# Router on unnormalised rows, modulation folded into its weights, reordered start, RWKV products and end

## The reference, cut to what matters

```python
mod = silu(c) @ w_ada + b_ada
sh1, sc1, gt1, sh2, sc2, gt2 = split(mod, 6)
h = rms_norm(x, norm1_g) * (1 + sc1) + sh1
y = hybrid_mixer(h, ...)          # RWKV-7 | mLSTM | window attention, gated, @ w_out
x = x + gt1 * y                   # x1 below
h = rms_norm(x, norm2_g) * (1 + sc2) + sh2
x = x + gt2 * hier_moe(h, ...)    # 32 experts, 4 groups, top 2 in the best group
# in hier_moe
g_prob   = softmax(h @ w_rg + b_rg);  g_top, g_idx = top_k(g_prob, 1)
e_logits = (h @ w_re + b_re).reshape(NT, 4, 8)   # those of group g_idx are used
```

## Time and profile before

| | before |
|---|---|
| median of 3 runs | 1950.85 us (1950.84 to 1951.01) |
| the profiled execution | 1950.37 us, its span 1948.6 us |
| PE busy | 1815.5 us, 93% of the span |
| DVE, ACT, POOL busy | 664.9, 438.4, 233.9 us |
| moved by DMA | 334.18 MB, mean 171 GB/s |
| the chain that ended last | PE 88%, DMA 4%, DVE 3%, ACT 2% |

### The profile page before, as it was taken

The page is one execution under the profiler, slowest core; times in us unless marked ns, Lnnn a source line. Parts: engine busy times, 40 slices in busy tenths (PEclk is TensorE's granted clock), DMA queues, the critical chain, the costliest instruction groups (busy, mean ns, idle before and its releaser), DMA issues.

```text
span 1948.6 us, 37426 instructions
## 1 busy us (share of the span) xinstructions
PE 1815.5 (93%) x16145; PEld 1014.4 (52%) x16145; DVE 664.9 (34%) x1569; ACT 438.4 (23%) x999; POOL 233.9 (12%) x352
## 2 busy tenths in 40 slices
PE   6999999999994999999999999996999999999990
PEld 3455445555442555555555554554566656655550
DVE  4385425554445233323332334553111001110014
ACT  4220412222334122211222131112222212222110
POOL 3030001000100122022201231001000000000003
PEclk9999999999997999999999999997999999999995
DMA  9386001001211001011010156224999999999988
GB/s 315 115 279 235 22 22 33 22 22 33 65 54 41 17 15 31 17 31 26 19 31 17 57 189 238 97 113 149 389 393 401 395 391 389 384 395 387 386 318 327
DMA packets 146930, 334.18 MB, mean 171 GB/s; under 512 B 19275, under 2 KB 63225, under 8 KB 146845
## 3 DMA queue, kind: packets, MB, share of 16 engines
q1 hardware_dynamic: 127776, 282.68, 40.0%
q0 software_dynamic: 8240, 25.04, 3.9%
q10 hardware_dynamic: 10828, 25.24, 3.3%
HBM read 299.50 MB, written 37.63 MB: 173 GB/s over the span
## 4 chain that ended last, share of the span: by engine, by line
PE 88%; DMA 4%; DVE 3%; ACT 2%; issue 1%; POOL 1%; SPq 1%; ACTq 0%; POOLq 0%; DVEq 0%
PE bank L285 83%; DMA arena<-in_w_e_in 3%; PE bank L1214 1%; POOL arena L718 1%; PE bank L885 1%; DMA arena<-y_slots,ints 1%; PE bank L1231 1%; SPq L457 0%; PE bank L1233 0%; PE bank L1153 0%; DMA y_slots<-arena 0%; DVE arena L1788 0%; DVE arena L1877 0%; PE bank L761 0%; ACT arena L1345 0%
## 5 line engine op out<-in xcount | busy, mean ns | idle before, releaser
L285 PE MATMUL bank<-arena 128*32 128x256 f32 (+8 forms) x15294 | 1726.3, 378 | 37.4 <-DVE arena L1877 6.3
L285 PEld LDWEIGHTS bank<-arena 128*32 128x32 f32 (+4 forms) x15294 | 924.8, 133 | 779.2 <-issue 522.5
L2232 DVE TENSOR_TENSOR arena<-arena,bank 128x128 f32<-128x128 f32 x96 | 21.9, 283 | 369.8 <-ACT arena L1631 369.8
L1618 ACT ACTIVATE arena<-bank,arena 128x96 f32<-128x96 f32 x256 | 85.9, 441 | 12.0 <-PE bank L1214 12.0
L682 POOL DMA_INDIRECT arena<-xnorm,ints x32 | 31.6, 986 | 471.1 <-PE bank L1214 466.7
L2241 DVE TENSOR_TENSOR arena<-bank,arena 128x512 f32<-128x512 f32 x64 | 35.7, 558 | 132.9 <-PE bank L285 132.9
L1624 ACT ACTIVATE arena<-bank 128x384 f32<-128x384 f32 x32 | 15.7, 490 | 267.7 <-PE bank L1233 267.7
L2025 DVE TENSOR_TENSOR arena<-arena,bank 128x256 f32<-128x256 f32 x40 | 16.8, 421 | 172.8 <-PE bank L285 172.8
L633 POOL TENSOR_TENSOR arena<-arena 64x256 f32<-64x256 f32 x96 | 71.2, 741 | 28.3 <-DVE arena L2011 21.7
L1569 ACT ACTIVATE arena<-bank 128x256 f32<-128x256 f32 (+1 forms) x48 | 18.3, 382 | 208.7 <-PE bank L285 208.7
L1631 ACT ACTIVATE arena<-bank 128x128 f32<-128x128 f32 x96 | 19.7, 278 | 164.6 <-PE bank L285 164.6
(11 more groups left out here) (330 smaller groups left out, 1013.2 us busy)
## 6 DMA issues: line engine op xcount, KB each, us to landing
arena<-in_w_e_in SPq DMA_DIRECT2D x64, 2048.0 KB, 22.1
arena<-in_w_e_out SPq DMA_DIRECT2D x32, 2048.0 KB, 22.1
arena<-in_w_ada SPq DMA_DIRECT2D x12, 2048.0 KB, 12.7
arena<-in_w_in SPq DMA_DIRECT2D x32, 512.0 KB, 3.9
y_slots<-arena ACTq DMA_DIRECT2D x32, 288.0 KB, 6.3
y_slots<-arena POOLq DMA_DIRECT2D x21, 384.0 KB, 17.5
arena<-in_x SPq DMA_DIRECT2D x4, 1024.0 KB, 8.3
arena<-in_w_in SPq DMA_DIRECT2D x2, 2048.0 KB, 25.0
```

The lines of the kernel that those rows point to most:

```text
L285: return nc.tensor.matmul(o, l, r, start=start, stop=stop)
L1618: ins = A.activation(e_xT[s][:, k, :], PS[k // 4][:, ts(k % 4, CAP)], ACT.Identity, scale=sc2[:, k:k + 1], bias=sh2[:, k:k + 1])
L2232: ins = TT(e_h[:, r, :], e_g[:, r, :], E_GU[r][:, P:2 * P], ALU.mult)
```

## The change

- Start: the copies of the transposed tiles 0 to 3 stand between ACT's squares; gate row 2 directly behind row 0; the copies of tiles 4 to 7 are all ACT's; DVE makes the products of slice 1 ahead of `norms(1)`.
- RWKV: the four products with `a_wr` together, then the four with `a_qs`.
- Router: transposes read `o_x` itself and wait for `o_x1`. `wr` is multiplied by `sc2` once; `ones` times (`wr` x `sh2`), eight matmuls in bank 2, is added to `br`; the norm factor `rstd` multiplies the logits. The copies to `o_hT` are plain. The update is added in two halves. SP's load into `o_x` also waits for the transposes.
- Tail: `place` and `table` of tile 6 before the last route; ranks of tile 6 in bank 0; the first two gathers read the table without a copy; DVE makes half of expert 0's `e_xT`.
- End: the x1 loads wait for `win_used` instead of `y`; POOL itself waits for the stores of y; ACT reads the number of extra blocks ahead of its last store.

```diff
@@ names
-        VECS, MOD1 = range(1, 3)
+        VECS, MOD1, WR_SHIFT, WR_SCALE, WR_BIAS = range(1, 6)
@@ rank_bank
-            return PS[6][:, 64:64 + NE] if t < NT - 1 else PS[4][:, 0:NE]
+            return PS[6][:, 64:64 + NE] if t < NT - 2 else PS[4 * (t - NT + 2)][:, 0:NE]
@@ sync
                     sp.wait_ge(sem("x_norm"), NT + t - 1)
+                    sp.wait_ge(sem("x_used"), NT + t - 1)
...
-            sp.wait_ge(sem("y"), 2 * (NE - 1))
+            sp.wait_ge(sem("win_used"), NE - 1)
             for t in range(NT):
                 sp.dma_start(f_x[t], x1_t[t]).then_inc(sem("gate_in"), 16)
@@ gpsimd, gather(e, s, wait)
-                G.tensor_copy(i_ix[s], i_tab[:, ds(e, 1)]).then_inc(sem("ix_set"), 1)
-                pool.wait_ge(sem("ix_set"), e + 1)
                 if wait:
+                    G.tensor_copy(i_ix[s], i_tab[:, ds(e, 1)]).then_inc(sem("ix_set"), 1)
+                    pool.wait_ge(sem("ix_set"), e - 1)
                     pool.wait_ge(sem("xs_used"), e - 1)
...
             pool.wait_ge(sem("extra_end"), 1)
+            for s in range(2):
+                pool.wait_ge(sem(f"y_st{s}"), 32 * NE // 2)
@@ tensor
             ada_row(0)
+            ada_row(2)
             for t in range(4, NT):
                 x_transposes(t)
-            ada_row(2)
...
-                for h in range(H):
-                    a, p = h % 2, h // 2
-                    rows = slice(64 * a, 64 * a + 64)
-                    mm(PS[3 + a][:, ts(p, N)], a_wr[rows, p, :], a_st[rows, p, :])
-                    ins = mm(PS[3 + a][rows, ts(2 + p, N)], a_qs[rows, p, :], a_st[rows, p, :])
+                for p in range(2):
+                    for a, rows in enumerate(halves):
+                        mm(PS[3 + a][:, ts(p, N)], a_wr[rows, p, :], a_st[rows, p, :])
+                for p in range(2):
+                    for a, rows in enumerate(halves):
+                        ins = mm(PS[3 + a][rows, ts(2 + p, N)], a_qs[rows, p, :], a_st[rows, p, :])
                 ins.then_inc(sem("a_Y"), 1)
...
             pe.wait_ge(sem("mix_done"), 2 * NT + NT)
+            pe.wait_ge(sem("setup_dve"), WR_SHIFT)
+            for k in range(KT):
+                ins = mm(PS[2][:, 0:36], ones, r_lg[:, k, :], k == 0, k == KT - 1)
+            ins.then_inc(sem("gates_pe"), 1)
...
             def transposes(t):
-                pe.wait_ge(sem("x_norm"), NT + t + 1)
+                pe.wait_ge(sem("o_x1"), t + 1)
...
             for t in range(NT):
+                if t == 0:
+                    pe.wait_ge(sem("setup_dve"), WR_BIAS)
...
             logits(NT - 1)
+            table(NT - 2)
             ranks(NT - 1)
...
-            table(NT - 2)
             table(NT - 1)
@@ scalar
             for t in range(4):
                 squares(t + 4)
+                x_out(t)
             A.activation(ss[:, 4:8], ss[:, 4:8], ACT.Sqrt, scale=1.0 / D, bias=EPS).then_inc(sem("x_ss"), 1)
-            for t in range(4):
-                x_out(t)
...
+                A.activation(o_hT[:, 0:4, :], PS[4].rearrange("p (k n) -> p k n", k=4), ACT.Copy).then_inc(sem("xT_a"), 1)
...
-            xT_out(0, 0)
+            xT_out(0, 0, 4)
...
-            store(NE - 1, 1)
-            for s in range(2):
-                act.wait_ge(sem(f"y_st{s}"), 32 * NE // 2)
             act.wait_ge(sem("router_dve"), EXTRAS)
             n_extra = act.value_load(i_ex[0:1, NX:NX + 1], min_val=0, max_val=NX)
             act.wait_ge(sem("slots_zero"), 16 * NX)
-            act.sem_inc(sem("extra_go"), 1)
+            store(NE - 1, 1)
@@ vector
-            norms(1)
             dve.wait_ge(sem("setup_act"), COND)
             ada(1)
-            for t in range(4, NT):
-                x_out(t)
+            norms(1)
             ada(3)
...
+            TT(r_lg, wr, bc(sh2, 36), ALU.mult).then_inc(sem("setup_dve"), 1)
+            dve.wait_ge(sem("setup_dve"), WR_SHIFT)
+            TT(wr, wr, bc(sc2, 36), ALU.mult).then_inc(sem("setup_dve"), 1)
...
+            dve.wait_ge(sem("gates_pe"), 5)
+            TT(br, br, PS[2][:, 0:36], ALU.add).then_inc(sem("setup_dve"), 1)
...
+                V.tensor_copy(o_hT[:, 4:8, :], PS[5].rearrange("p (k n) -> p k n", k=4)).then_inc(sem("xT_v"), 1)
+                if t == NT - 1:
+                    place(NT - 2)
                 dve.wait_ge(sem("r_mm"), t + 1)
-                TT(r_lg[:, t, :], PS[6][:, 0:36], br, ALU.add).then_inc(sem("r_lg"), 1)
+                STT(r_lg[:, t, :], PS[6][:, 0:36], rstd[:, t:t + 1], br, ALU.mult, ALU.add).then_inc(sem("r_lg"), 1)
```

More of the change, by code:

```diff
@@ L1266, in _ @@
             pe.wait_ge(sem("xs1_in"), 16)
-            pe.wait_ge(sem("e_xT"), 1)
             xT(1, 1)
@@ L1348, in x_out @@
                 act.wait_ge(sem("x_used"), t + 1)
-                A.activation(HT[:, 0:4, ts(t, P)], PS[2 * (t % 2)].rearrange("p (k n) -> p k n", k=4), ACT.Copy)\
-                    .then_inc(sem("xT_a"), 1)
+                for j in range(1 if t < 4 else 2):
+                    ins = A.activation(HT[:, 4 * j:4 * j + 4, ts(t, P)], PS[2 * (t % 2) + j].rearrange("p (k n) -> p k n", k=4), ACT.Copy)
+                ins.then_inc(sem("xT_a"), 1)
             for t in range(4):
@@ L2163, in _ @@
             route(NT - 1)
-            place(NT - 2)
             place(NT - 1)
@@ L2241, in y_out @@
                     TT(e_y[s][:, cols], PS[5 + u][:, 0:(512, 256)[u]], gt2[:, cols], ALU.mult).then_inc(sem("y_out"), 1)
+            dve.wait_ge(sem("xs_used"), 1)
+            for k in range(4, KT):
+                ins = TS(e_xT[0][:, k, :], PS[1][:, ts(k - 4, CAP)], sc2[:, k:k + 1], sh2[:, k:k + 1], ALU.mult, ALU.add)
+            ins.then_inc(sem("xT_v"), 1)
             activate(0)
```

57 lines of the change are left out of this document (32 added, 25 removed).

## The result

The changed kernel takes 1920.2 us (median of 6 runs, 1918.35 to 1921.95), the kernel before 1950.8 (median of 6, 1948.54 to 1951.01): ratio 0.9848, 95% interval 0.9839 to 0.9858. Forecast were 1927.9 and a range of 1924 to 1936. The profiled execution took 1921.71 us, its span 1919.8; that of before 1950.37 and 1948.6. The table cuts both spans at the same seven events, so a stretch is the time from one event to the next. Its times are starts of rows of PE's, SP's and POOL's timelines and of the chain of waits, before and after.

A forecast was written before the change was run, and what follows sets the result against it. PE was taken to bound the chunks, w_out loop and experts, a chain over several engines the router tail and end. -3.4 - 12.0 + 3.55 - 0.8 - 4.7 - 5.6 = -22.95 gave 1927.9 us as median, range 1924 to 1936.

The forecast's parts named there:

- What bounds the kernel: PE is busy nearly throughout RWKV chunks, w_out loop and experts, so its savings there move the end one for one.
- Part 2: RWKV chunks: grouped state products take 0.96 us instead of 2.47 per chunk, 1.5 x 8 chunks, -12.0 us.
- rival A: RWKV chunks: `a_wr` products do not overlap, or only form changes are saved; -4.9 to -8, 1932 to 1935; chance 0.12.
- all terms at their better ends: Whole kernel: every term comes out at its favourable bound, giving 1924 us; chance 0.04.
- Rival C: Merges and on: narrow matmuls and short stalls leave PE's clock at 1.2 GHz; slower, 1976 us; chance 0.03.
- A clock of 0.5 in the merges: Merges after the RWKV chunks: PE showing this granted clock would mean the forecast is wrong.
- Part 1: Start, up to the first projection: gate row 0 starts at 22.4 us instead of 25.87, -3.4 us.
- Part 3: Router weights, merges to w_out: eight added matmuls +2.0, waits +0.35 and +1.2, sum +3.55 us; separately -0.8 in the loop.
- The shorter copies were covered too: w_out loop: plain copies to `o_hT` save nothing, because w_out matmuls already hide them.
- Part 4: Router tail, last w_out matmul to first expert matmul: -2.5, -0.7, -0.3 and -1.2, sum -4.7 us.
- Part 5: End: last store of y lands sooner without x1 loads beside it, -4.5, ACT's part -1.1; sum -5.6 us.
- Loads of the experts: Experts: DMA share is 1.03, but PE's progress releases the loads, so they move with PE's start.

The follow-up runs named there:

- state_undone: The changed kernel with the old order of the state products (`a_wr` and `a_qs` alternating) in the RWKV chunks: 1938.19 us, ratio 0.9941 to the kernel before.
- state_alone: The kernel before with only the new order of the state products (four `a_wr`, then four `a_qs` per RWKV chunk): 1929.13 us, ratio 0.9890.
- narrow_split: The kernel before, old order kept, with two of eight 512-column matmuls moved from behind the state products to ahead of them: 1949.10 us, ratio 0.9998.

## Why the prediction was wrong

**What bounds the kernel.** Right that the chunks move the end one for one. The failing step stands here: the row 638 to 1146 us has a clock of 0.98, and I read only its busy column. A mean of 0.98 over 508 us is 0.02 x 508 = 10 us of full-speed work lost. The five falls are 17 us at 1.2 GHz, which is 8.5 us of it; the rest is the end of the slow stretch ahead of chunk 1, and rounding.

**Part 2.** The term "-12.0" was right for what it priced, 8 x 1.50, and rival A is out: the products with `a_wr` do run in pairs. The term was mis-sized, because it left out that the removed stretch also cost the clock behind it, which the sum put at nothing. The chunks gave 19.5 us in this trace, 7.5 more than the term; by the totals it is 6.0 (state_undone, 18.0 - 12.0) to 9.2 (state_alone, 21.2 - 12.0). That is why the time lies below the range. The range was also cut short by its own terms: -14 for `a_wr` at 0.045 comes to 13.2 by the figures beside it, and all terms at their better ends give about 1922, not 1924. Even so, 1920.2 lies below. The 2.50 us were read in chunk 8, where the clock fell some 1 us behind the end of my window. Rival C had the clock only as a risk of the new work. A fall did come behind the narrow matmuls at 1120 us in this trace, but it cost 1.7 us and did not last through the merges. A clock of 0.5 in the merges was among the signs of a wrong forecast, and it came. Whether these matmuls bring it is not shown: it is in four of nine traces that have them there, and in one of seven that have not (narrow_split).

**Up to chunk 1**, forecast 0, measured -2.60: two falls of the kernel before are shorter or missing (0.8 us of the first projections; 1.5 of the first attention products, 9.06 us instead of 10.52), and the chain ahead of chunk 1 is 0.4 shorter. The fall at the attention products is in eight of sixteen traces, with the change and without, so it belongs to the execution, not to the change.

**Part 1**, -3.4: measured -3.42, and the match is luck. Row 0 starts at 21.20, not at 22.4, and takes 7.03 us, not 8.07; row 2 then waits 2.31 us for its slice of w_ada, which comes as late as 30.54, not at 29.2. The two misses meet at the forecast start of row 2, 30.5. Over all traces the first projection starts at 46.9 to 50.3 with the change (mean 48.0 of 12) and 50.1 to 51.5 without (mean 50.7 of 4): -2.8 in the mean.

**Part 3**, +3.55: measured +4.69. The 0.35 us wait for wr*sh2 cost nothing, since PE waited 0.65 there before as well; 2.0 for the matmuls; 0.93 for the bias instead of 1.2; 1.7 for the fall, without which the stretch would be below the forecast. In the w_out loop 2.0 were saved instead of 0.8: each tile's row is 0.15 shorter (16.57 for 16.72), 1.0 in seven tiles. "The shorter copies were covered too" was wrong by that: in the kernel before ACT's last copy to `o_hT` ends at 1232.23 and the first logits matmul starts at 1232.28, right behind it, 0.15 later than the matmul ahead of it would let it; with the change the copies end at 1191.95 and that matmul starts at 1192.78.

**Part 4**, -4.7: measured -4.5, by the ends of the last w_out rows (1310.03 and 1287.16) and the first expert matmul. Right. Behind it expert 0's first half took 1.0 longer, clock again.

**Part 5**, -5.6: the store -4.8, ACT's part -1.1, together -5.9; a fall ahead of expert 31's last products, 7.07 instead of 5.39, gave 1.7 back. The gathers' +1.6 is within what the traces show among themselves (37.3 to 39.2 us from the first gather to the end).

**Loads of the experts** "move with PE's start": true of the start, and incomplete: the DMA engines set a floor of some 549 us behind expert 0's first half, so a gain inside the experts would hardly have counted. By the same floor the fall at expert 1 costs this kernel little: the stretch takes 550.2 us, with the kernel before, which has no such fall, at 550.1.

## What to carry to other kernels

Read the clock column before the busy column: a mean of 0.98 over a long stage can be the largest item in it, and where two equal iterations differ in length, ask why before you price one. On TensorE, put matmuls of one tile form together; single matmuls of changing forms, on one half of the array at a time, cost their own length and may cost clock behind them. Before filling a wait with useful work, ask which chain binds next; and where nothing useful fits, idle matmuls ahead of a dense stretch can be worth more than the stall they fill.

## What the runs showed that was not expected

- The granted clock can fall while PE shows no idle time at all: behind 2.5 us of serially issued 64-row matmuls, in two to five of eight chunks in each of the four traces with the old order; in none of the twelve traces with products of one form side by side, even at 2.9 us of such work.
- The halves of the array run side by side within a group of one form whatever the order inside it (60.94 and 60.92 us); a change of form costs 0.15 us.
- Seven idle matmuls, 14 instructions, brought 6.2 us, some 5 of them in the stage where they stand.
- The runs of one kernel lie 1.8 to 9.8 us apart, and the traces differ by single falls, most of 1.7 us of work, at weak places: 31 us, 266 us, the merges, expert 1, expert 31. Effects of 1 to 2 us are to be read in the stage, not in the total.
